# GpSimd's split of the chunks behind each half of a differential attention, held until VectorE's last weighted sum

## The chip, the cores and the metric

The kernel runs on one core of a Trainium2 chip. The metric is the device time of one launch in microseconds.

## The reference

Two transformer blocks are computed for 512 tokens of width 1024, all in float32. The first block has sliding-window attention, a gated delta rule, an MLP and a gated embedding. The second block has retention, differential attention, a merge by gates, an output projection, and a mixture of 32 experts with two per token. The change lies in the differential attention of the second block, whose core is:

```python
def block(args):
    i, qi = args
    s = jnp.einsum('bqhcd,bkhcd->bhcqk', qi, k).astype(jnp.float32) * scale
    qpos = i * Q_BLOCK + jnp.arange(Q_BLOCK)
    s = jnp.where(kpos[None, :] <= qpos[:, None], s, neg)
    p = jax.nn.softmax(s, axis=-1)
    a = p[:, :, 0] - lam * p[:, :, 1]
    return jnp.einsum('bhqk,bkhe->bqhe', a.astype(v.dtype), v)
```

There are 4 heads, each with two score matrices (c = 0, 1) of dk 128 and values of width 256, and four blocks of 128 queries. The queries, keys, values and two gates are projections of the same normalized input by `w_in_2` (1024 by 8192). After the attention, each head is normalized and multiplied by `w_diff_o_2`.

## The kernel before

**Weights in chunks.** Every dense product ("linear") of the first part of the kernel works on chunks of a weight matrix: 512 rows by 512 columns, laid out as 128 partitions by 2048 values, 1 MB. SyncE loads a chunk into one of three raw buffers (`load_chunk`, L233). Float32 precision comes from splitting each value into a high part and a low part: `split_chunk` does it on GpSimd, the high part `whi` at L241, and the low part `wlo` as raw minus high at L243. There are two buffers of `whi` and `wlo` (PAIR = 2). TensorE then makes three matmuls for each product (`three`, L264 to L266). In the MLP and some other places ScalarE and VectorE do the splits, but in the phase of the change GpSimd does all of them.

The order of chunks is fixed in one list. The load of chunk n waits until chunk n-3 is split. The split of chunk n waits until the load has landed and until TensorE is done with chunk n-2 (`used`), since it takes its buffer. `stream_split(pool, upto)` splits all chunks up to `upto + 2`, excluding that one, that have not been split yet.

**The differential attention** is done in two halves of two heads each. The chunks of a half are, in order: two for the queries FQ, two for the keys FK, two for the values FV (`U_dif[half][0]`), and then two for the gate (`gd_chunks[half]`); `U_dif[half][1]` is the index of the first gate chunk. Behind the gate chunks of the first half come FQ of the second, and behind those of the second half the four chunks of `w_diff_o_2` and then those of `w_out_2`.

In `attention(half)` each engine runs through eight units j = 0 to 7 (two heads, and in each four query blocks n = 0 to 3, with (n+1)*128 keys):

- TensorE: `scores` (one matmul for each of the two score matrices, into PSUM, L1958), issued two units ahead; pieces of the gate product, which use the two gate chunks, between units (done in unit 5); `turn` (n+1 transposes of the weighted probabilities, L1970), which waits for VectorE's weighted sum of this unit and for ScalarE's copy of the unit before; and after n = 3 `values` (16 matmuls, L1985).
- VectorE: `maxima`, one unit ahead: causal mask (L2146), maximum (L2149), scaling of two numbers per partition (L2151). Then for the unit itself: reciprocal of the sums (L2160), times lambda (L2162), first matrix scaled (L2163), and the weighted sum (L2166), which counts up the semaphore `dif` to step "a".
- ScalarE: exponentials one unit ahead (L2070), and behind them the copy of the turned probabilities out of PSUM (L2081); between units a copy of a gate tile (L2057). Its queue runs in order: the exponentials of unit j+1 stand before the copy of unit j.

Units count on through the halves: unit 7 of a half is `dif.at("a", 8 * half + 7)`.

When the units of the first half are done, TensorE goes on to the FQ linear of the second half, and behind the second half to the linear of `w_diff_o_2` (`U_do[0]`). Each begins with its first chunk: 48 matmuls, then the second chunk. The matmuls of the head's mean square (L2012) are put in after its first 12 matmuls. VectorE and ScalarE then normalize the half's heads (L1864 to L1879).

**Queues in this phase.** GpSimd's program is a single `stream_split(pool, out_end)`: it splits as soon as loads and buffers allow. SyncE loads the chunks up to the one behind the gate chunks, writes 16 blank blocks of 512 KB to `y_rows` (L1756), and goes on with loads.

Of the kernel before, what the change touches and what calls it, by code (L numbers as in the profile page):

```python
# [127 lines left out]
def build(nc, IN, out):  # L128
    ctx = ExitStack()
    with ctx:  # L130
# [14 lines left out]
        def late(name):  # L145

            late_sems.append(late_ctx.enter_context(nc.semaphore(name)))
            return late_sems[-1]
# [86 lines left out]
        def split_chunk(pool, n):  # L235
            _, rows, cols = chunks[n]
            w, r, s = rows * cols, n % RAW, n % PAIR
            pool.wait_ge(raw_full[r], 16 * (n // RAW + 1))
            if n >= PAIR:
                pool.wait_ge(*used[n - PAIR])  # L240
            nc.gpsimd.tensor_scalar(whi[:, s, 0:w], raw[:, r, 0:w], 1.0, 1.0, ALU.mult, ALU.mult).then_inc(split_hi, 1)  # L241
            pool.wait_ge(split_hi, n + 1)
            nc.gpsimd.tensor_tensor(wlo[:, s, 0:w], raw[:, r, 0:w], whi[:, s, 0:w].bitcast(F32),  # L243
                                    ALU.subtract).then_inc(split_done, 1)

        def chunk_high(act, n):

            _, rows, cols = chunks[n]
            w, r, s = rows * cols, n % RAW, n % PAIR
            act.wait_ge(raw_full[r], 16 * (n // RAW + 1))  # L250
            if n >= PAIR:
                act.wait_ge(*used[n - PAIR])
            nc.scalar.activation(whi[:, s, 0:w], raw[:, r, 0:w], ACT.Copy).then_inc(split_hi, 1)  # L253

        def chunk_low(dve, n):

            _, rows, cols = chunks[n]
            w, r, s = rows * cols, n % RAW, n % PAIR
            dve.wait_ge(split_hi, n + 1)
            nc.vector.tensor_tensor(wlo[:, s, 0:w], raw[:, r, 0:w], whi[:, s, 0:w].bitcast(F32), ALU.subtract).then_inc(split_done, 1)  # L260
# [107 lines left out]
        U_dif, U_gd, gd_chunks = [], [], []  # L368
# [27 lines left out]
        def stream_in(sp, upto_chunk):  # L396
            while issued[0] < min(upto_chunk + RAW, len(chunks)):
                load_chunk(sp, issued[0])
                issued[0] += 1

        def stream_split(pool, upto_chunk):
            while done_split[0] < min(upto_chunk + PAIR, len(chunks)):
                split_chunk(pool, done_split[0])
                done_split[0] += 1
# [92 lines left out]
        with phase() as block:  # L497
            @block.sync
            def _(sp):
                sp.dma_start(cbase[:], IN["k_base"][:, 0:4 * P]).then_inc(consts_in, 16)  # L500
                for t in range(TT):
                    sp.dma_start(x_tok[:, t, :], IN["x"][0, t * P:t * P + P, :]).then_inc(x_in, 16)
                stream_in(sp, 0)
# [1344 lines left out]
        dif = Steps(late("dif_dve"), "inv", "lam", "a0", "a")  # L1848
# [53 lines left out]
        with phase() as block:  # L1902
# [18 lines left out]

            @block.gpsimd
            def _(pool):
                stream_split(pool, out_end)

            @block.tensor
# [987 lines left out]
```

## Time and profile before

| | |
|---|---|
| median of 3 runs | 2122.1 us (2116.88, 2122.1, 2130.04) |
| profiled execution, own time | 2120.33 us |
| its span | 2118.5 us |
| mean granted TensorE clock | 0.969 |
| TensorE (PE) busy | 93%, 1974.1 us |
| VectorE (DVE) busy | 64%, 1361.0 us |
| ScalarE (ACT) busy | 44%, 939.1 us |
| GpSimd (POOL) busy | 25%, 534.8 us |
| DMA | 388.51 MB, mean 183 GB/s |

The span runs from the first to the last instruction in the profile; times in the rows are counted from its start. PEclk is the granted TensorE clock as a share of 2.4 GHz: 1.00 is 2.4 GHz and 0.50 is 1.2 GHz. A timeline row has the start, the duration, engine, line and operation, output<-inputs with shapes, the count of merged instructions, and in brackets the idle time of the engine just before it with what ended that. A wait row has who waited for whom, with the total, the count and the longest.

### The profile page before, as it was taken

The page shows a single profiled execution, that of the slowest core. Times are in us where ns is not written, and L with a number is a line of the kernel's source. Part 1 is how long each engine was busy: PE and PEld are TensorE (multiplying, and loading weights), DVE is VectorE, ACT ScalarE, POOL GpSimd, SP SyncE. Part 2 cuts the span into 40 slices and gives each one's busy share as a digit, 9 for nine tenths or more (in the row PEclk, how much of TensorE's full clock was granted, in tenths as well). Part 3 has the DMA queues.
Part 4 walks back from the last instruction along what each step waited for, and adds up shares of the span by engine and source line. Part 5 has one row for each costly group of instructions (what it writes and reads, how often), then busy time and mean ns, then how long its engine had stood idle before and what let it go on. Part 6 is the DMA issues. An engine that isn't in the chain of part 4 may idle for free. (4 is left out here: it accounts for less than half of the span.)

```text
span 2118.5 us, 24193 instructions
## 1 busy us (share of the span) xinstructions
PE 1974.1 (93%) x8966; PEld 1588.8 (75%) x8966; DVE 1361.0 (64%) x1393; ACT 939.1 (44%) x1029; POOL 534.8 (25%) x274
## 2 busy tenths in 40 slices
PE   3997898999999999999999897999999999999993
PEld 2875786888888877768877575778788787787882
DVE  4437874667665556524025446547799899999994
ACT  3113425423223452232002313325788888878883
POOL 2633003100000004516553353430022222222222
PEclk7998999999999999999999898998999999999996
DMA  4221001565563232243335153212899999999994
GB/s 146 96 90 60 21 14 40 189 194 200 173 207 135 96 93 74 69 160 100 100 99 219 42 185 131 79 64 111 302 376 373 364 363 366 367 378 375 371 363 152
DMA packets 115163, 388.51 MB, mean 183 GB/s; under 512 B 21333, under 2 KB 23668, under 8 KB 88334
## 3 DMA queue, kind: packets, MB, share of 16 engines
q1 hardware_dynamic: 98656, 353.00, 46.0%
q10 hardware_dynamic: 10382, 25.42, 3.6%
q0 software_dynamic: 6048, 9.03, 1.2%
q8 instruction: 52, 0.85, 0.2%
q14 instruction: 25, 0.20, 0.0%
HBM read 355.06 MB, written 45.35 MB: 189 GB/s over the span
## 5 line engine op out<-in xcount | busy, mean ns | idle before, releaser
L2832 DVE TENSOR_TENSOR m_lo<-m_raw,m_hi 128x2048 fp32r<-128x2048 f32 x200 | 449.1, 2286 | 9.4 <-ACT m_hi L2754 9.0
L2754 ACT ACTIVATE m_hi<-m_raw 128x2048 fp32r<-128x2048 f32 x200 | 383.1, 1922 | 105.1 <-DMA m_raw<-in_w_exp_gate_dram 67.0
L264 PE MATMUL ps<-xhi,whi 128*128 128x512 f32 x936 | 375.6, 401 | 11.8 <-DVE xlo L455 6.7
L265 PE MATMUL ps<-xlo,whi 128*128 128x512 f32 x936 | 366.2, 391 | 0.0
L266 PE MATMUL ps<-xhi,wlo 128*128 128x512 f32 x936 | 366.1, 391 | 0.0
L241 POOL TENSOR_SCALAR whi<-raw 128x2048 fp32r<-128x2048 f32 (+1 forms) x60 | 113.6, 1894 | 953.5 <-PE ps L266 874.9
L243 POOL TENSOR_TENSOR wlo<-raw,whi 128x2048 fp32r<-128x2048 f32 (+1 forms) x60 | 277.0, 4616 | 5.0
L264 PE MATMUL ps<-m_hi,xt_hi 128*128 128x512 f32 x544 | 218.6, 402 | 6.2 <-DVE xt_lo L2837 5.0
L264 PEld LDWEIGHTS ps<-xhi,whi 128*128 128x128 f32 x936 | 176.7, 189 | 57.4 <-issue 15.7
L265 PE MATMUL ps<-m_lo,xt_hi 128*128 128x512 f32 x544 | 215.7, 396 | 0.0
L266 PE MATMUL ps<-m_hi,xt_lo 128*128 128x512 f32 x544 | 214.0, 393 | 0.0
L265 PEld LDWEIGHTS ps<-xlo,whi 128*128 128x128 f32 x936 | 177.0, 189 | 39.2 <-issue 3.4
L266 PEld LDWEIGHTS ps<-xhi,wlo 128*128 128x128 f32 x936 | 176.8, 189 | 37.4
L264 PE MATMUL ps<-yhi,whi 128*128 128x512 f32 x448 | 175.8, 392 | 0.0
L266 PE MATMUL ps<-yhi,wlo 128*128 128x512 f32 x448 | 174.4, 389 | 0.0
L265 PE MATMUL ps<-ylo,whi 128*128 128x512 f32 x448 | 174.3, 389 | 0.0
L260 DVE TENSOR_TENSOR wlo<-raw,whi 128x2048 fp32r<-128x2048 f32 (+1 forms) x38 | 84.9, 2234 | 114.3 <-ACT whi L253 114.3
L253 ACT ACTIVATE whi<-raw 128x2048 fp32r<-128x2048 f32 (+1 forms) x38 | 70.9, 1867 | 167.5 <-PE ps L266 115.6
L264 PEld LDWEIGHTS ps<-m_hi,xt_hi 128*128 128x128 f32 x544 | 101.9, 187 | 32.5 <-issue 8.7
L266 PEld LDWEIGHTS ps<-m_hi,xt_lo 128*128 128x128 f32 x544 | 102.7, 189 | 24.2
L265 PEld LDWEIGHTS ps<-m_lo,xt_hi 128*128 128x128 f32 x544 | 102.5, 188 | 22.5
L2675 POOL TENSOR_TENSOR p_col<-p_col 128x1 f32<-128x1 f32 x34 | 47.2, 1388 | 283.8 <-ACT y_out L2773 283.8
(474 smaller groups left out, 3181.6 us busy)
## 6 DMA issues: line engine op xcount, KB each, us to landing
m_raw<-in_w_exp_gate_dram SPq DMA_DIRECT2D x68, 1024.0 KB, 5.9
m_raw<-in_w_exp_up_dram SPq DMA_DIRECT2D x68, 1024.0 KB, 6.4
m_raw<-in_w_exp_down_dram SPq DMA_DIRECT2D x68, 1024.0 KB, 5.9
raw<-in_w_in_dram SPq DMA_DIRECT2D x42, 1024.0 KB, 5.2
ada_w<-in_w_ada_dram ACTq DMA_DIRECT2D x48, 512.0 KB, 4.2
raw<-in_w_up_dram SPq DMA_DIRECT2D x16, 1024.0 KB, 5.7
raw<-in_w_down_dram SPq DMA_DIRECT2D x16, 1024.0 KB, 5.0
y_rows<-xhi SPq DMA_DIRECT2D x32, 512.0 KB, 11.4
```

Of the source, the lines that this page charges most:

```text
L241: nc.gpsimd.tensor_scalar(whi[:, s, 0:w], raw[:, r, 0:w], 1.0, 1.0, ALU.mult, ALU.mult).then_inc(split_hi, 1)
L243: nc.gpsimd.tensor_tensor(wlo[:, s, 0:w], raw[:, r, 0:w], whi[:, s, 0:w].bitcast(F32), ALU.subtract).then_inc(split_done, 1)
L253: nc.scalar.activation(whi[:, s, 0:w], raw[:, r, 0:w], ACT.Copy).then_inc(split_hi, 1)
L260: nc.vector.tensor_tensor(wlo[:, s, 0:w], raw[:, r, 0:w], whi[:, s, 0:w].bitcast(F32), ALU.subtract).then_inc(split_done, 1)
L264: nc.tensor.matmul(o, lh, rh, start=start, stop=False)
L265: nc.tensor.matmul(o, lh, rl, start=False, stop=False)
L266: return nc.tensor.matmul(o, ll, rh, start=False, stop=stop)
L2675: nc.gpsimd.tensor_tensor(p_col[:, 2:3], p_col[:, 0:1], p_col[:, 1:2], ALU.add)
L2754: nc.scalar.activation(m_hi[s][:], m_raw[s][:], ACT.Copy).then_inc(m_split, 1)
L2832: nc.vector.tensor_tensor(m_lo[s][:], m_raw[s][:], m_hi[s][:].bitcast(F32), ALU.subtract).then_inc(m_low, 1)
```

## The change

Before it splits everything up to the end of the phase, GpSimd goes through the two halves: it splits up to and including the two gate chunks of the half, and then waits until VectorE has made the weighted sum of unit 7 of that half. Only then does it go on to the chunks behind them: FQ of the second half behind the first, `w_diff_o_2` behind the second. All other engines' programs are as before.

```diff
--- before.py
+++ after.py
@@ -1921,6 +1921,9 @@
 
             @block.gpsimd
             def _(pool):
+                for half in range(2):
+                    stream_split(pool, U_dif[half][1])
+                    pool.wait_ge(*dif.at("a", 8 * half + 7))
                 stream_split(pool, out_end)
 
             @block.tensor
```

## Rows read from the trace of the kernel before

**Rows 1.** Waits of TensorE, whole span: total us, times, longest us
```profile
PE ps L1970 <- DVE dif_p L2166: 17.8, 2, 8.9
```

**Rows 2.** Timeline of VectorE, units 6 and 7: start us, us, engine, line
```profile
1175.52 1.23 DVE L2149 TENSOR_REDUCE dif_v<-ps 128x2 f32<-128x1024 f32 x1
1176.78 3.13 DVE L2151 TENSOR_SCALAR dif_v<-dif_v 128x2 f32<-128x2 f32 x1
...
1180.01 1.74 DVE L2162 TENSOR_TENSOR dif_v<-dif_v,small 128x1 f32<-128x1 f32 x1
...
1182.12 4.73 DVE L2166 SCALAR_TENSOR_TENSOR dif_p<-dif_p,dif_v 128x384 f32<-128x384 f32 x1
...
1187.55 0.75 DVE L2166 SCALAR_TENSOR_TENSOR dif_p<-dif_p,dif_v 128x512 f32<-128x512 f32 x1
```

**Rows 3.** Timeline of GpSimd, first half: three splits (of the third its start)
```profile
1173.35 1.90 POOL L241 TENSOR_SCALAR whi<-raw 128x2048 fp32r<-128x2048 f32 x1 [27.67 <-PE ps L266]
1175.33 4.55 POOL L243 TENSOR_TENSOR wlo<-raw,whi 128x2048 fp32r<-128x2048 f32 x1
1179.85 1.90 POOL L241 TENSOR_SCALAR whi<-raw 128x2048 fp32r<-128x2048 f32 x1
1181.83 4.60 POOL L243 TENSOR_TENSOR wlo<-raw,whi 128x2048 fp32r<-128x2048 f32 x1
1209.40 1.91 POOL L241 TENSOR_SCALAR whi<-raw 128x2048 fp32r<-128x2048 f32 x1 [22.97 <-PE ps L266]
```

**Rows 4.** Timeline of TensorE, first half: transposes of unit 7, value products, next linear
```profile
1188.48 1.09 PE L1970 MATMUL ps<-cbase,dif_p 128*128 128x128 f32 x4 [0.67 <-ACT dif_t L2081]
1190.25 6.31 PE L1985 MATMUL ps<-dif_t,fv 128*128 128x512 f32 x16 [0.69 <-ACT dif_t L2081]
1196.32 0.48 PE L264 MATMUL ps<-xhi,whi 128*128 128x512 f32 x1
```

**Rows 5.** Timeline of ScalarE, first half: gate copy, exponentials of unit 7
```profile
1178.32 0.59 ACT L2057 ACTIVATE gd_sig<-ps 128x512 f32<-128x512 f32 x1
1179.94 0.69 ACT L2070 ACTIVATE dif_p<-ps,dif_v 128x512 f32<-128x512 f32 x1 [1.03 <-DVE dif_v L2151]
...
1181.19 0.20 ACT L2070 ACTIVATION_READ_ACCUMULATOR dif_p<-ps,dif_v 128x1 f32 x1
```

**Rows 6.** Timeline of VectorE, then TensorE, units 2 and 3, without splits beside
```profile
1150.12 1.23 DVE L2149 TENSOR_REDUCE dif_v<-ps 128x2 f32<-128x1024 f32 x1
...
1152.17 0.62 DVE L2166 SCALAR_TENSOR_TENSOR dif_p<-dif_p,dif_v 128x384 f32<-128x384 f32 x1
...
1154.09 0.17 DVE L2160 RECIPROCAL dif_v<-dif_v 128x2 f32<-128x2 f32 x1 [0.29 <-ACT dif_p L2070]
...
1154.88 0.75 DVE L2166 SCALAR_TENSOR_TENSOR dif_p<-dif_p,dif_v 128x512 f32<-128x512 f32 x1
...
1158.83 0.60 PE L1970 MATMUL ps<-cbase,dif_p 128*128 128x128 f32 x4
1160.11 4.58 PE L1985 MATMUL ps<-dif_t,fv 128*128 128x512 f32 x16 [0.69 <-ACT dif_t L2081]
1164.45 0.47 PE L264 MATMUL ps<-xhi,whi 128*128 128x512 f32 x1
```

**Rows 7.** Timeline of TensorE, second half: transposes of unit 7, next linear
```profile
1320.12 1.08 PE L1970 MATMUL ps<-cbase,dif_p 128*128 128x128 f32 x4 [0.67 <-ACT dif_t L2081]
...
1328.68 0.48 PE L264 MATMUL ps<-yhi,whi 128*128 128x512 f32 x1
```

**Rows 8.** Windows: length, busy us of each engine, granted clock, DMA share, GB/s
```profile
342.00:344.00 2.00, 0.00 (x0) 0.00 (x0) 0.49 (x1) 1.95 (x3) 0.00 (x0) 0.96 0.00 0
1178.00:1187.00 9.00, 0.10 (x2) 0.10 (x2) 8.89 (x7) 2.32 (x6) 8.35 (x3) 0.62 0.38 117
```

**Rows 9.** DMA issues from 1120 to 1230 us: KB each, us to landing
```profile
y_rows<-xhi SPq DMA_DIRECT2D x16, 512.0 KB, 11.6
raw<-in_w_in_dram SPq DMA_DIRECT2D x7, 1024.0 KB, 5.3
```

## The prediction

> **What bounds the kernel now.** I read the page first: TensorE is busy for 93% of the span, so what counts is what TensorE waits for. The view of waits, for TensorE over the whole span, has one entry that belongs to this change: its transposes at L1970 wait 17.8 us in all, in two waits of up to 8.9 us, for VectorE's weighted sum at L2166 [rows 1]. Then I read each engine's timeline around the first of the two.
>
> In the first half VectorE does its last row of maxima over 512 columns at 1175.52 us. Then L2151, which touches 2 numbers per partition, takes 3.13 us and ends at 1179.91; L2162 takes 1.74 us and ends at 1181.75; the weighted sum of unit 6 takes 4.73 us and ends at 1186.85; that of unit 7 ends at 1188.30 [rows 2]. GpSimd works beside it: the low part (L243) that ends at 1179.88, the high part (L241) that ends at 1181.75, the next low part that ends at 1186.43 [rows 3]. VectorE's ends follow GpSimd's by 0.03, 0.00 and 0.42 us, and 0.42 us is what is left of a sum that by itself takes 0.62 us [rows 6]. So two engines that share no semaphore here end together three times. These GpSimd instructions are the splits of the two chunks behind the half, and the first of them was released by TensorE at 1173.35 [rows 3]: exactly what the change holds back. TensorE meanwhile is busy for 0.10 us of the 9 between 1178 and 1187 [rows 8]. What follows on it is a chain without slack: transposes of unit 6, of unit 7, the value products, then the next linear, which starts at 1196.32 [rows 4]. The second half repeats this 131.64 us later (1320.12 for 1188.48), and its next linear starts at 1328.68 [rows 4, 7].
>
> **The change, part by part.** It adds two waits on GpSimd; no instruction of work is added or removed. Per half, the two gate chunks are still split as before, since the helper splits two chunks beyond its argument. Behind each wait are queued the two splits above and all later ones; who needs them is TensorE's next linear, and SyncE's loads, which go by the count of splits.
>
> *The stall removed.* With GpSimd silent, unit 6's sum would end 2.67 us after the start of the 512-column maximum, as in unit 2 of the same half (1150.12 to 1152.79 [rows 6]), at 1178.2. That isn't what limits then. ScalarE's queue is next: its gate copy ends at 1178.91, and only behind it come the exponentials of unit 7, 1.45 us (1179.94 to 1181.39) [rows 5], to 1180.36. VectorE needs 0.04 us to start and 1.54 us from the reciprocal to the end of the sum (1154.09 to 1155.63 [rows 6]): unit 7's sum ends at 1181.94 in place of 1188.30. TensorE began 0.18 us after it [rows 2, 4], so its last transposes start at about 1182.0 in place of 1188.48: 6.48 us earlier. Unit 6's transposes and copy fit in before that.
>
> *From there to the next linear.* This depends on TensorE's clock. In the first half of the kernel before it took 1196.32 - 1188.48 = 7.84 us, in the second 1328.68 - 1320.12 = 8.56 us [rows 4, 7]. The same work for the first head of the half took 1164.45 - 1158.83 = 5.62 us [rows 6]; its value products took 4.58 us against 6.31 us [rows 4, 6]. The granted clock explains it: from 1178 to 1187 us, with hardly a matmul under way, the mean is 0.62, that is the engine began at 2.4 GHz and fell to 1.2 GHz [rows 8], and the value products began at the lower level. After the change TensorE still has about 5.3 us, from 1178.0 to the value products at 1183.3 (1.28 us behind the start of the last transposes, as in the first head [rows 6]), with unit 7's 0.60 us of transposes in them and the three of unit 6, some 1.1 us together. A pause of 2 us already brought the beginning of a fall (342 to 344 us, no matmul, mean 0.96 [rows 8]). So I expect the fall again, and take the stretch at its measured lengths: next linear at 1182.0 + 7.84 = 1189.8, or + 8.56 = 1190.6.
>
> By the Trainium skill, "TensorE: Matmul & The Clock Gate", Part 1, the clock goes by how busy the array has lately been and comes back only after sustained work. By that rule the fall is still to be expected here and the sum would be the 13 us below; if two short bursts of transposes kept the clock up, it would be the 15.7 us of the first rival. The rows decide it no further than that they show falls in pauses like this one.
>
> *The split that now comes late.* GpSimd starts when unit 7's sum is done. High and low part of one chunk take 6.58 us from start to end (1179.85 to 1186.43 [rows 3]); with 0.18 us to wake and 0.1 us to release TensorE the first chunk is there at 1181.94 + 6.86 = 1188.8. TensorE's own work covers it until 1189.8 in the slow-clock case, so it costs nothing; at the high clock TensorE would be there at 1182.0 + 5.62 = 1187.6 and wait 1.2 us. The second chunk is there at about 1195.4. TensorE needs it only when it is done with the first: 48 matmuls, and GpSimd's third split, which waits for just that, started at 1209.40 [rows 3], 13.1 us behind the linear's start. So it has until about 1202.9. VectorE has nothing to do in this time, so the splits run beside nobody. From the third split on everything hangs on the linear's start and moves with it. Bounds for the unseen cost of the wait: nothing, or 1.2 us a half; I take nothing.
>
> *Loads.* The load of the chunk five behind the first gate chunk is released by the delayed split, at about 1188.8; a load lands in 5.3 us [rows 9], and this chunk is split only behind the third split, which comes some 14 us after the release. Hidden.
>
> *Sum.* First half 6.5 us (1196.32 to 1189.8; 5.8 at the longer stretch). Second half, the same shift: 6.5 us with its own stretch of 8.56, 7.2 with 7.84. Together 12.3 to 13.7 us; if the clock falls late, so that the transposes still run fast and only the value products are slow, the start of the products is 0.5 us earlier in each half, up to 14.7. I take 13.5 us. All later stages hang on TensorE through these linears, so nothing absorbs it. The profiled execution took 2120.3 us (span 2118.5 and 1.8 around it): 2120.3 - 13.5 = 2106.8, say 2107. The median of the runs shown is 1.8 us higher, which would make 2108.6; the runs themselves lie 13 us apart, so I keep 2107.
>
> **The rivals.**
> 1. *The clock stays up.* The pauses are broken by transposes, and the longest, before those of unit 7, is about 3.0 us. Then the linears start when the split is done, at 1188.8 and 131.64 us later at 1320.4: 7.5 + 8.2 = 15.7 us, 2104.6; one half of the two gives 14.7. The new bound would be GpSimd's split. Against it: the fall that begins before 344 us, in a shorter pause.
> 2. *The stall doesn't go.* If VectorE's long instructions came from something else, unit 7's sum would still end at 1188.30, the split at 1195.2, and TensorE at 1196.3 would notice nothing: 2120. Against it: three coincident ends, the same in the second half.
> 3. *Slower: the raw chunk isn't there when GpSimd's wait ends*, so that a load stands on the path before L241. Break-even is when the first chunk is ready at 1196.3, 14.3 us after unit 7's sum; with 6.86 us for wait and split this decides at 7.5 us of loading. An ordinary load of 5.3 us would leave a gain of 2 to 3 us a half; one that takes the 11.6 us of the writes of y_rows on the same queue [rows 9] costs 4.1 us in the first half and 3.4 in the second, 7.5 in all: 2127.8. Against it: the split before was released by TensorE, not by a DMA [rows 3], so the chunk was already there, and nothing of SyncE's order changes.
>
> **How the numbers follow.** Forecast 0.58, rival 1 0.27, rival 2 0.10, rival 3 0.05. A measurement of this kernel tells about 1% (21 us) from no change. No case gives that much: the largest gain is 15.7 us, and only a spread of runs like the one shown could carry it over 21 us, 0.06. Slower by over 1% needs a load longer than 11.6 us: 0.02. Within 1%: 0.92. The forecast's own range is 2106 to 2108 by the terms; with rival 1 and the runs' scatter of a few us on both sides the range is 2100 to 2115; rivals 2 and 3 are left out.
>
> **What would show it.** Right: GpSimd's first split behind a half starts within 0.3 us of the end of unit 7's sum; no L2151, L2162 or L2166 in units 6 and 7 above 0.8 us; TensorE's waits for L2166 shrink from 17.8 us to below 3 us, and a wait for ScalarE's exponentials or of about 3 us before unit 7's transposes takes their place; clock rows below 1.0 again in the value products; last transposes to linear 7.8 to 8.6 us. It is wrong if the sums stay long with GpSimd silent, if TensorE waits at the linear for GpSimd's L243 by more than about 1 us, or if the gain at the linears is lost in a later stage.

## The result and the profile after

The changed kernel takes 2107.29 us, the median of 7 runs (2104.34 to 2115.27); the kernel before took 2120.05 us in the 7 runs beside them (2116.88 to 2130.04). The ratio is 0.9928 with a 95% interval of 0.9907 to 0.9949: by the ratio it is 15 us faster, within 11 to 20, which is less than 1%. The forecast was 2107.0 us. The profiled execution took 2113.64 us (span 2111.8).

The waits of TensorE over the whole span, which answer to [rows 1]; the columns are the total, the count and the longest. All lines behind L1923 have moved down by 3, so L1970 is now L1973 and the weighted sum L2166 is L2169:

```profile
PE ps L1973 <- DVE dif_p L2169: 5.6, 2, 2.8
```

17.8 us have become 5.6, in two waits of 2.8. VectorE's timeline for units 6 and 7 of the first half, which answers to [rows 2]:

```profile
1175.42 1.23 DVE L2152 TENSOR_REDUCE dif_v<-ps 128x2 f32<-128x1024 f32 x1
1176.68 0.17 DVE L2154 TENSOR_SCALAR dif_v<-dif_v 128x2 f32<-128x2 f32 x1
...
1177.48 0.62 DVE L2169 SCALAR_TENSOR_TENSOR dif_p<-dif_p,dif_v 128x384 f32<-128x384 f32 x1
1180.18 0.17 DVE L2163 RECIPROCAL dif_v<-dif_v 128x2 f32<-128x2 f32 x1 [2.09 <-ACT dif_p L2073]
...
1180.97 0.75 DVE L2169 SCALAR_TENSOR_TENSOR dif_p<-dif_p,dif_v 128x512 f32<-128x512 f32 x1
```

Every instruction has the length that it had in units 2 and 3 [rows 6]; the scaling took 0.17 us there too. The scaling of two numbers takes 0.17 us in place of 3.13, and the weighted sums take 0.62 and 0.75 us in place of 4.73 and 0.75. Unit 7's sum ends at 1181.72 us. The reciprocal at 1180.18 now waits 2.09 us for ScalarE. GpSimd, which answers to [rows 3]:

```profile
1181.81 1.90 POOL L241 TENSOR_SCALAR whi<-raw 128x2048 fp32r<-128x2048 f32 x1 [36.22 <-DVE dif_p L2169]
1183.79 4.50 POOL L243 TENSOR_TENSOR wlo<-raw,whi 128x2048 fp32r<-128x2048 f32 x1
1188.26 1.90 POOL L241 TENSOR_SCALAR whi<-raw 128x2048 fp32r<-128x2048 f32 x1
1190.24 4.58 POOL L243 TENSOR_TENSOR wlo<-raw,whi 128x2048 fp32r<-128x2048 f32 x1
1202.84 1.91 POOL L241 TENSOR_SCALAR whi<-raw 128x2048 fp32r<-128x2048 f32 x1 [8.01 <-PE ps L266]
```

The first split starts 0.09 us behind the sum and ends at 1188.29, the second ends at 1194.82, the third starts at 1202.84, when TensorE has released the first chunk. TensorE in the first half, from the transposes of unit 5 on, which answers to [rows 4]:

```profile
1177.52 0.38 PE L1973 MATMUL ps<-cbase,dif_p 128*128 128x128 f32 x2
1178.46 0.52 PE L1973 MATMUL ps<-cbase,dif_p 128*128 128x128 f32 x3 [0.56 <-ACT dif_t L2084]
1181.78 1.11 PE L1973 MATMUL ps<-cbase,dif_p 128*128 128x128 f32 x4 [2.79 <-DVE dif_p L2169]
1183.58 6.41 PE L1988 MATMUL ps<-dif_t,fv 128*128 128x512 f32 x16 [0.69 <-ACT dif_t L2084]
1189.74 0.48 PE L264 MATMUL ps<-xhi,whi 128*128 128x512 f32 x1
```

The next linear starts at 1189.74 with no wait of its own: the split was there 1.45 us earlier. The value products still take 6.41 us. The windows show why; their columns are those of [rows 8]:

```profile
1178.00:1182.00 4.00, 0.74 (x4) 0.54 (x5) 1.56 (x5) 2.53 (x7) 0.19 (x1) 0.81 0.00 0
1182.00:1186.00 4.00, 3.31 (x7) 1.66 (x7) 0.00 (x0) 0.60 (x1) 3.92 (x2) 0.50 0.02 4
1186.00:1188.00 2.00, 2.00 (x7) 1.35 (x6) 0.00 (x0) 0.00 (x0) 2.00 (x1) 0.67 0.00 0
1188.00:1190.00 2.00, 2.00 (x9) 1.34 (x8) 0.00 (x0) 0.00 (x0) 2.00 (x2) 1.00 0.31 48
```

The clock falls to 1.2 GHz before 1182 us, in the pause of 2.79 us ahead of unit 7's transposes, and is back at 2.4 GHz by 1188; the products run without a gap from 1183.58 on, so the first of them run at the lower level. ScalarE's queue, which answers to [rows 5], shows what now comes last before unit 7's sum, the gate copy and then the exponentials:

```profile
1178.22 0.59 ACT L2060 ACTIVATE gd_sig<-ps 128x512 f32<-128x512 f32 x1
1178.69 0.69 ACT L2073 ACTIVATE dif_p<-ps,dif_v 128x512 f32<-128x512 f32 x1
```

**Where the time went, by stages.** One length is used in all that follows: from the start of unit 5's transposes (the ones with two per group, L1970 or L1973) to the start of the next linear. It was 18.70 us in the first half of the kernel before (1177.62 to 1196.32) and 19.42 in the second; it is 12.22 (1177.52 to 1189.74) and 12.76 us (1302.71 to 1315.47) in the changed one. A second length runs from that same point of the first half to the mixture's first load. It was 1426.59 - 1177.62 = 248.97 us and is 1413.42 - 1177.52 = 235.90 us: 13.07 us less, of which the two halves give 6.48 and 6.66. So nothing between the attention and the mixture takes anything back. The row of unit 5's transposes in the kernel before, from TensorE's timeline, and then its loads, from SyncE's queue:

```profile
1177.62 0.38 PE L1970 MATMUL ps<-cbase,dif_p 128*128 128x128 f32 x2
...
1426.59 0.90 SPq L2319 DMA_DIRECT2D m_raw<-in_w_exp_gate_dram  x2
...
1488.74 3.13 SPq L2319 DMA_DIRECT2D m_raw<-in_w_exp_up_dram  x2
...
2059.68 0.44 SPq L2661 DMA_DIRECT2D mod_g<-mod_hold  x1
```

The loads of the changed kernel:

```profile
1413.42 0.91 SPq L2322 DMA_DIRECT2D m_raw<-in_w_exp_gate_dram  x2
...
1475.53 3.10 SPq L2322 DMA_DIRECT2D m_raw<-in_w_exp_up_dram  x2
...
2052.80 0.43 SPq L2664 DMA_DIRECT2D mod_g<-mod_hold  x1
```

The mixture itself, from its second group of loads (behind a stretch of 59 us without loads) to the load of its gate, took 577.27 us in this execution (1475.53 to 2052.80) and 570.94 in that of before (1488.74 to 2059.68). That is why the profiled spans differ by only 6.7 us while the medians differ by 12.8. Two of the runs below look at this.

### The profile page after: what moved, and what is told of

It reads as the page before. It is cut to its first block and busy times, and to the rows that moved or that the text cites. A ratio compares the mean times of both kernels' runs of the same rounds, so it can differ in the third digit from the quotient of the medians.

```text
span 2111.8 us, 24193 instructions
## 1 busy us (share of the span) xinstructions
PE 1980.2 (94%) x8966; PEld 1593.8 (75%) x8966; DVE 1343.4 (64%) x1393; ACT 939.0 (44%) x1029; POOL 533.1 (25%) x274
## 5 line engine op out<-in xcount | busy, mean ns | idle before, releaser
L260 DVE TENSOR_TENSOR wlo<-raw,whi 128x2048 fp32r<-128x2048 f32 (+1 forms) x38 | 84.9, 2234 | 114.2 <-ACT whi L253 114.2
L253 ACT ACTIVATE whi<-raw 128x2048 fp32r<-128x2048 f32 (+1 forms) x38 | 71.0, 1867 | 167.4 <-PE ps L266 115.6
L264 PE MATMUL ps<-m_hi,ht_hi 128*128 128x512 f32 x272 | 107.2, 394 | 1.8 <-ACT y_out L2776 1.8
```

The costliest lines, as they stand in the source:

```text
L264: nc.tensor.matmul(o, lh, rh, start=start, stop=False)
```

## The experiments

There were twelve runs beside the two of the comparison: ten other kernels, and each of the two once more. "Half 1" and "half 2" are the first length, "to mixture" the second, "products" the value products of unit 7 in the two halves, "mixture" the length of the mixture as just given. The ratio is to the runs of the kernel before beside them. A kernel is "filled" where matmuls whose result nobody reads stand in one of TensorE's pauses. The cuts of code show only the lines in question, against the changed kernel, or against the kernel before where no wait on GpSimd is in it; "..." marks lines left out.

| kernel | half 1 | half 2 | products | to mixture | mixture | ratio (95%) |
|---|---|---|---|---|---|---|
| before | 18.70 | 19.42 | 6.31, 7.03 | 248.97 | 570.9 | |
| changed | 12.22 | 12.76 | 6.41, 6.95 | 235.90 | 577.3 | 0.9928 (0.9907 to 0.9949) |
| first wait alone | 12.18 | 19.44 | 6.36, 7.05 | 242.49 | 577.7 | 0.9968 (0.9951 to 0.9985) |
| second wait alone | 18.71 | 12.71 | 6.33, 6.90 | 242.36 | 574.2 | 0.9959 (0.9944 to 0.9973) |
| wait for the products | 18.50 | 18.43 | 6.28, 6.21 | 251.81 | 575.5 | 1.0021 (1.0002 to 1.0040) |
| wait for unit 6 | 22.07 | 22.80 | 6.28, 7.01 | 255.75 | 566.9 | 1.0027 (1.0009 to 1.0046) |
| changed, pause filled | 10.83 | 10.84 | 4.58, 4.58 | 232.59 | 576.2 | 0.9925 (0.9905 to 0.9945) |
| the same, gate copy late | 10.35 | 10.35 | 4.58, 4.58 | 231.63 | 572.7 | 0.9937 (0.9917 to 0.9958) |
| split on idle engines | 9.45 | 9.45 | 4.58, 4.58 | 229.79 | 572.4 | 0.9915 (0.9889 to 0.9941) |
| before, 8 behind unit 6 | 24.02 | 23.80 | 4.58, 4.58 | 258.73 | 568.2 | 1.0056 (1.0032 to 1.0081) |
| before, 8 behind unit 5 | 18.81 | 19.38 | 6.50, 7.27 | 249.10 | 573.4 | 0.9982 (0.9962 to 1.0003) |
| before, 10 behind unit 5 | 16.43 | 16.44 | 4.58, 4.58 | 244.05 | 572.6 | 0.9994 (0.9972 to 1.0016) |
| before, again | 18.80 | 19.46 | 6.40, 7.06 | 249.16 | 567.1 | 1.0003 (0.9983 to 1.0023) |
| changed, again | 12.12 | 12.71 | 6.31, 6.90 | 235.72 | 573.5 | 0.9932 (0.9902 to 0.9962) |

In both kernels that were run twice the length up to the mixture repeats within 0.2 us, and the halves within 0.1, so these lengths resolve what the whole kernel's time, which scatters by 9 to 20 us between runs of one kernel, doesn't.

**One wait alone, in either half.**

```diff
-                for half in range(2):
-                    stream_split(pool, U_dif[half][1])
-                    pool.wait_ge(*dif.at("a", 8 * half + 7))
+                stream_split(pool, U_dif[0][1])
+                pool.wait_ge(*dif.at("a", 7))
                 stream_split(pool, out_end)
```

> Only the first half's wait. Read as the time from the start of unit 5's transposes to the start of the next linear (before: 18.70 us in the first half, 19.42 in the second; changed kernel: 12.22 and 12.82). Theory (GpSimd's split stretches VectorE's small instructions): first half 12 to 12.5, second half still 19 to 19.8, whole kernel 6.5 us below before. Rival (something else in the changed order shortens both, or the stall of the second half depends on the first): second half also changes. Rival (a later stage takes part of it back): less than 6.5 at the start of the mixture's loads.

> Only the second half's wait. Theory: first half still 18 to 19 us from unit 5's transposes to the next linear, second half 12.5 to 13.2; the start of the mixture's loads 6.6 us earlier than before; whole kernel 6.6 us below before, and with the run of the first half alone the two gains add up to the changed kernel's. Rival: the two do not add up.

In the second of them the index is 1 and the unit 15. Each wait shortens its own half and leaves the other as it was: 12.18 and 19.44, 18.71 and 12.71. To the mixture they save 6.48 and 6.61 us, 13.09 together, against 13.07 for both. The ratios give 6.8 and 8.7 us, and 15 for both. The halves are independent and add up, as the theory had it. (The expectation gives 12.82 us for the changed kernel's second half; its trace has 12.76.)

**The wait put later, behind the value products.**

```diff
-                    pool.wait_ge(*dif.at("a", 8 * half + 7))
+                    pool.wait_ge(dif_value, 2 * half + 2)
```

> The wait is put later: GpSimd goes on only when the half's last value products are done. Nothing covers the split then, and TensorE should stand at the next linear for 0.2 + 6.5 + 0.1 = 6.8 us in each half. Theory (the split in the changed kernel is covered by the last transposes and value products): from unit 5's transposes to the next linear 12.2 + 6.8 = 19.0 us and 12.8 + 6.8 = 19.6, so the kernel lies at before's time, within 1 us. A pause this long should also pull the clock down again at the linear's start, at 1 to 2.5 us more a half, so up to 5 us slower than before. Rival (the split is not what the next linear needs): time as the changed kernel.

TensorE's timeline at the next linear of the first half:

```profile
1182.00 6.28 PE L1988 MATMUL ps<-dif_t,fv 128*128 128x512 f32 x16 [0.69 <-ACT dif_t L2084]
1194.90 0.80 PE L264 MATMUL ps<-xhi,whi 128*128 128x512 f32 x1 [6.62 <-POOL wlo L243]
```

Now TensorE stands for GpSimd's low part, 6.62 us in each half. So the split is indeed what the next linear needs, and in the changed kernel it is the products that cover it. The clock comes down again in this wait, as expected: it is granted at 1.00 from 1188 to 1192 us and at a mean of 0.59 from 1192 to 1195. The window behind the linear's start:

```profile
1195.00:1199.00 4.00, 4.00 (x10) 3.14 (x11) 0.00 (x0) 0.00 (x0) 3.92 (x2) 0.50 0.74 220
```

The halves were expected at 19.0 and 19.6 us and came out at 18.50 and 18.43: the transposes of unit 7 ran at the high clock in both, in 0.66 us, and in the second half the products took 6.21 us in place of 6.95. But to the mixture it is 2.84 us more than before although the halves are 0.20 and 0.99 us shorter, so 4.0 us are lost behind the linears' starts, which begin at 1.2 GHz. Held until nothing covers the split, the same wait loses what it had gained: the kernel is at 1.0021 (1.0002 to 1.0040) of the kernel before.

**The wait put earlier, at unit 6's sum.**

```diff
-                    pool.wait_ge(*dif.at("a", 8 * half + 7))
+                    pool.wait_ge(*dif.at("a", 8 * half + 6))
```

> The wait is put earlier: GpSimd goes on at the weighted sum of unit 6, about 3.7 us before that of unit 7. Theory (an instruction of VectorE with operands in SBUF stands until GpSimd's instruction ends): the first low part runs from about 1180.1 to 1184.6 us; unit 7's reciprocal or product before it stretches to that end, the sum of unit 7 ends at about 1186 in place of 1181.7, possibly later if it meets the second split too, and the next linear starts 4 to 7 us later than in the changed kernel in each half. Rival (VectorE is only slowed in proportion, or only the long weighted sums suffer): less than 1 us later. Rival (the early split helps, since it is done sooner): faster than the changed kernel.

VectorE from unit 7's reciprocal on, and GpSimd beside it, in the first half:

```profile
1179.94 0.17 DVE L2163 RECIPROCAL dif_v<-dif_v 128x2 f32<-128x2 f32 x1 [2.09 <-ACT dif_p L2073]
1180.14 4.29 DVE L2165 TENSOR_TENSOR dif_v<-dif_v,small 128x1 f32<-128x1 f32 x1
1184.36 2.21 DVE L2166 TENSOR_SCALAR dif_p<-dif_p,dif_v 128x512 f32<-128x512 f32 x1
1186.60 4.86 DVE L2169 SCALAR_TENSOR_TENSOR dif_p<-dif_p,dif_v 128x512 f32<-128x512 f32 x1
```

```profile
1177.94 1.90 POOL L241 TENSOR_SCALAR whi<-raw 128x2048 fp32r<-128x2048 f32 x1 [32.61 <-DVE dif_p L2169]
1179.92 4.50 POOL L243 TENSOR_TENSOR wlo<-raw,whi 128x2048 fp32r<-128x2048 f32 x1
1184.39 1.90 POOL L241 TENSOR_SCALAR whi<-raw 128x2048 fp32r<-128x2048 f32 x1
1186.37 4.54 POOL L243 TENSOR_TENSOR wlo<-raw,whi 128x2048 fp32r<-128x2048 f32 x1
```

Three instructions in a row stand: the product of one number per partition for 4.29 us, to 1184.43, where the low part ends at 1184.42; the scaling of the first matrix to 1186.57, past the end of the high part at 1186.29; the weighted sum to 1191.46, past the end of the next low part at 1190.91. One number per partition stands as long as a matrix, so it is no slowing in proportion. The second half shows the same three lengths, 4.29, 2.21 and 4.86 us. I had expected the sum at 1186 or later; it met the second split too and came at 1191.46. The halves take 22.07 and 22.80 us: 3.4 us longer each than with no wait at all, and the kernel is slower than before by 0.27%. In the kernel before unit 6's sum took the worst of it, and unit 7 was free; here, with the splits started 3.6 us earlier than in the changed kernel, the whole of unit 7 behind its reciprocal is caught.

The prediction named no rival in which the DMA traffic that runs beside the splits holds VectorE up. The windows settle it. They lie within the scaling of 3.13 us in the kernel before, and within the product of 4.29 us in this one:

```profile
1176.80:1179.80 3.00, 1.20 (x7) 0.75 (x5) 3.00 (x1) 0.87 (x2) 3.00 (x1) 1.00 0.00 0
```

```profile
1180.20:1184.40 4.20, 0.00 (x0) 0.00 (x0) 4.20 (x2) 0.09 (x1) 4.20 (x2) 0.85 0.00 0
```

The DMA share, the last column but one, is 0.00 in both, while VectorE and GpSimd are busy from end to end.

By the Trainium skill, "SBUF — State Buffer", "SBUF: two separate sides", VectorE and GpSimd share a pair of ports to SBUF as an exclusive lock, held for the whole instruction. The three ends here agree with it. That page names VectorE's instructions with two inputs in SBUF or in a two-port mode. The rows fit: the product and the weighted sum have two such inputs and stood, and the reciprocal at 1179.94, which has one and ran within the low part, took its usual 0.17 us. The scaling has one input and stood too; by that page this takes the two-port mode, and no row here shows in which mode it ran.

**TensorE's pause filled.** Three matmuls go in before unit 7's transposes; their result is read by nobody and they are no part of the computation.

```diff
                         turn(j)
+                        if j == 6:
+                            pe.wait_ge(dif_exp, 2 * (i0 + 7))
+                            for _ in range(3):
+                                nc.tensor.matmul(ps[:, SB, :], ident, fk[:, 0, :], start=True, stop=True)
```

> The changed kernel, and TensorE fills the pause before unit 7's transposes with three matmuls whose result nobody reads (some 2.8 us at 2.4 GHz). Theory (the value products run at 1.2 GHz only because of the pause): the granted clock stays at 1.0 and the products take 4.6 us, not 6.4 and 6.95; TensorE then stands for GpSimd's first split, since this is ready at 6.8 us after unit 7's sum: next linear 1.0 to 1.5 us earlier than in the changed kernel in the first half, 1.5 to 2 in the second, 2.5 to 3.5 us in all, and a wait for L243 of about 1 us. Rival (the clock falls for another reason): products as long as before and nothing gained. Rival (the filling delays unit 7's transposes): up to 0.5 us a half lost.

```profile
1183.60 2.74 PE L2008 MATMUL ps<-fk,cbase 128*128 128x512 f32 x6
1186.56 0.66 PE L1973 MATMUL ps<-cbase,dif_p 128*128 128x128 f32 x4 [0.21 <-DVE dif_p L2173]
1187.90 4.58 PE L1988 MATMUL ps<-dif_t,fv 128*128 128x512 f32 x16 [0.69 <-ACT dif_t L2088]
1193.13 0.50 PE L264 MATMUL ps<-xhi,whi 128*128 128x512 f32 x1 [0.65 <-POOL wlo L243]
```

The granted clock is 1.00 from 1183 to 1196 us, the products take 4.58 us in both halves, and TensorE stands 0.65 and 0.66 us for the low part. The halves are 1.39 and 1.92 us shorter than in the changed kernel, 3.31 us in all to the mixture. So in the changed kernel the pause is what brings the clock down, and with it gone GpSimd's split is the bound, as the first rival of the forecast said. The whole kernel's ratio (0.9925) can't tell this from the changed kernel (0.9928).

**The clock in the kernel before.** Three tries with the same unread matmuls and no wait on GpSimd; in the first j is 6 and there are 8, in the second and third j is 5 and there are 8 and 10.

```diff
                         turn(j)
+                        if j == 5:
+                            pe.wait_ge(dif_exp, 2 * (i0 + 7))
+                            for _ in range(10):
+                                nc.tensor.matmul(ps[:, SB, :], ident, fk[:, 0, :], start=True, stop=True)
```

> The kernel before, with no wait on GpSimd, and the 8.9 us pause filled with eight matmuls whose result nobody reads (7.5 us at 2.4 GHz). It takes the clock's share by itself. Theory: VectorE's long instructions stay (3.1, 1.7 and 4.7 us), the clock stays at 1.0, the stretch from unit 7's transposes to the next linear shrinks from 7.84 and 8.56 us to 5.6, so 2.2 + 2.9 = 5 us faster than before in all. Rival (the low clock is no consequence of the pause): no change.

This one was put in the wrong place: in the kernel before the long pause lies ahead of unit 6's transposes, not behind them, so the eight matmuls stood on the path for 8.58 us and the kernel got slower. One reading it gives all the same: with them, unit 7's transposes to the linear took 1203.92 - 1198.30 = 5.62 us.

> The kernel before, without a wait on GpSimd, with the eight unread matmuls now where its 8.9 us pause is: behind the transposes of unit 5, before those of unit 6 (in the run with them behind unit 6 they came after the pause, on the path). Theory (the pause brings the clock down): VectorE's long instructions stay, the value products take 4.6 us, and from unit 5's transposes to the next linear it takes 18.70 - 0.4 - 2.2 = about 16 us in the first half and 19.42 - 0.4 - 2.9 = about 16 in the second. From the first half's unit 5 to the mixture's first load some 5.5 us less than before's 248.97. Rival (the clock is low for another cause): 18.7 and 19.4 as before.

```profile
1179.31 7.03 PE L2005 MATMUL ps<-fk,cbase 128*128 128x512 f32 x16
1188.39 0.63 PE L1970 MATMUL ps<-cbase,dif_p 128*128 128x128 f32 x3 [2.05 <-DVE dif_p L2170]
1189.84 1.12 PE L1970 MATMUL ps<-cbase,dif_p 128*128 128x128 f32 x4 [0.83 <-DVE dif_p L2170]
1191.64 6.50 PE L1985 MATMUL ps<-dif_t,fv 128*128 128x512 f32 x16 [0.69 <-ACT dif_t L2085]
```

```profile
1188.00:1190.00 2.00, 0.79 (x4) 0.47 (x5) 1.71 (x5) 0.49 (x1) 0.00 (x0) 0.68 0.44 72
```

Nothing was gained. Eight matmuls took 7.03 us and left a pause of 2.05, and the products took 6.50 us in the first half and 7.27 in the second. By an estimate from the mean clock of windows that hold the change of level, it fell in the first half 0.3 us behind the pause (0.68 from 1188 to 1190), and in the second, behind a pause of the same length, only 1.7 us behind it (0.71 from 1321 to 1323), when unit 7's transposes were under way. So the fall doesn't come at a fixed distance from the pause.

> As the run with eight unread matmuls behind unit 5 in the kernel before, but with ten, some 8.8 us, so that nothing of the first pause is left. With eight a pause of 2.05 us stayed, and the value products ran at 1.2 GHz (6.50 and 7.27 us). Theory (a pause of 2 us followed by short transposes with waits between them is enough for the low clock): value products 4.6 us, unit 7's transposes to the next linear 5.6 us, so 16.5 us from unit 5's transposes to the next linear in both halves, and 244 us from unit 5 to the mixture's first load (before 248.97). Rival (in the kernel before the clock falls for a cause other than the pause): 18.7 and 19.4 again.

```profile
1177.11 8.75 PE L2005 MATMUL ps<-fk,cbase 128*128 128x512 f32 x20
1186.19 0.55 PE L1970 MATMUL ps<-cbase,dif_p 128*128 128x128 f32 x3 [0.34 <-DVE dif_p L2170]
1187.64 0.66 PE L1970 MATMUL ps<-cbase,dif_p 128*128 128x128 f32 x4 [0.91 <-DVE dif_p L2170]
1188.98 4.58 PE L1985 MATMUL ps<-dif_t,fv 128*128 128x512 f32 x16 [0.69 <-ACT dif_t L2085]
1193.32 0.48 PE L264 MATMUL ps<-xhi,whi 128*128 128x512 f32 x1
```

With ten the pause is 0.34 us, the products take 4.58 us, and the halves 16.43 and 16.44, to the mixture 244.05, as expected. The granted clock is 1.00 in every window from unit 5's transposes to the linear, with gaps of 0.34, 0.91 and 0.69 us. So of the kernel before the clock's share was 2.3 and 3.0 us a half. The ratio of this kernel, 0.9994 (0.9972 to 1.0016), doesn't show the 4.9 us; in its profiled execution the stage from the mixture's first load to its second group of loads took 66.6 us in place of 62.1. The changed kernel got none of it: it takes away 6.5 us of standing and leaves a pause that still costs the clock. By the Trainium skill, "TensorE: Matmul & The Clock Gate", Part 1, activity releases the clock and idleness throttles it; these runs agree with that, and here a pause of 2.05 us with short transposes behind it was already followed by the fall.

**ScalarE's queue.** Two unread matmuls, and the copy of the last gate tile (L2060) behind the copy of unit 6.

```diff
-                        elif j == 5:
+                        elif j == 6:
                             gate_out(half, 3)
```

> The changed kernel with the pause filled by two matmuls and, on ScalarE, the last gate tile's copy moved from before unit 7's exponentials to behind the copy of unit 6. Theory (unit 7's exponentials, and with them its sum and GpSimd's start, hang on ScalarE's queue): they start about 0.5 us earlier, sum, split and next linear with them; together with the fuller clock 1.5 to 2 us a half below the changed kernel, 3 to 4 us in all. Rival (the exponentials wait for something else): nothing beyond what the filled pause gives, 2.5 to 3.5 us.

Both halves take 10.35 us, 0.48 less than with the pause filled alone. Unit 7's exponentials begin 0.70 us behind unit 5's transposes (1186.44 for 1185.74) and not 1.17 (1183.47 for 1182.30), so they did hang on that copy. That there are two unread matmuls here and three there takes no part in it: in both TensorE waits for unit 7's sum behind them, 0.59 and 0.21 us. To the mixture the kernel is 4.27 us below the changed one, a little more than the 3 to 4 expected; its ratio, 0.9937, doesn't show it.

**The first split on the engines that are idle.** ScalarE makes the high part behind the copy of unit 6, VectorE the low part behind unit 7's sum, with the helpers that the MLP uses (`chunk_high`, L253; `chunk_low`, L260). The two unread matmuls stay. `done_split` is the program's own count of split chunks: raised by one, it makes GpSimd leave that chunk out and go on when the others have split it.

```diff
-                        elif j == 5:
+                        if j == 6:
+                            chunk_high(act, U_dif[half][1] + 2)
+                        elif j == 7:
                             gate_out(half, 3)
...
+                    chunk_low(dve, U_dif[half][1] + 2)
...
                     stream_split(pool, U_dif[half][1])
-                    pool.wait_ge(*dif.at("a", 8 * half + 7))
+                    done_split[0] += 1
+                    pool.wait_ge(split_done, done_split[0])
```

> The first chunk behind each half is no longer split by GpSimd but by two engines that stand idle then: ScalarE makes the high part behind the copy of unit 6, VectorE the low part behind the sum of unit 7; GpSimd goes on when that is done. The last gate copy stands behind the copy of unit 7, and two unread matmuls fill TensorE's pause. Theory (what is left behind the changed kernel's sum is GpSimd's 6.5 us and a pause with low clock): chunk ready 2.5 to 3 us after the sum, TensorE goes to the linear without a wait: 9.4 us from unit 5's transposes to the next linear in both halves (changed kernel 12.22 and 12.76, kernel with the late gate copy 10.35), and 229.5 to 230 us from unit 5 of the first half to the mixture's first load (changed 235.9). Rival (the new work on ScalarE's or VectorE's queue delays the copy of unit 7 or the sum): 10.3 us or more.

```profile
1187.88 0.75 DVE L2176 SCALAR_TENSOR_TENSOR dif_p<-dif_p,dif_v 128x512 f32<-128x512 f32 x1
1189.27 2.29 DVE L260 TENSOR_TENSOR wlo<-raw,whi 128x2048 fp32r<-128x2048 f32 x1 [0.64 <-ACT whi L253]
```

```profile
1190.03 4.58 PE L1989 MATMUL ps<-dif_t,fv 128*128 128x512 f32 x16 [0.69 <-ACT dif_t L2089]
1194.37 0.48 PE L264 MATMUL ps<-xhi,whi 128*128 128x512 f32 x1
```

The chunk is there at 1191.56, 2.9 us behind the sum's end at 1188.63, and TensorE goes from the products into the linear with nothing between. The halves take 9.45 us each, so 9.3 and 10.0 us less than before, and 229.79 us to the mixture: 19.2 us less than before and 6.1 less than the changed kernel. The ratio, 0.9915 (0.9889 to 0.9941), beats the kernel before; against the changed kernel run beside it (0.9932, 0.9902 to 0.9962) the intervals overlap, so there only the stage shows it ahead.

**Both kernels once more.**

> The kernel before, once more, for a second trace of it. If the mixture's length (from the second group of its loads to the gate's load at its end: 570.9 us before, 577.3 in the changed kernel) differs only from execution to execution, this one may lie anywhere in 567 to 578. If the changed kernel makes the mixture longer, it lies at 571 within 2 us. From unit 5 to the mixture's first load: 249.0 within 0.3.

> The changed kernel once more. Scatter of executions: mixture anywhere in 567 to 578 us. The change at fault: 577 within 2 us. From unit 5 to the mixture's first load 235.9 within 0.6 (the clock may come back one step earlier or later). Ratio to before 0.993 to 0.994.

Up to the mixture they repeat: 249.16 us and 235.72. The mixture took 567.1 and 573.5 us. The changed kernel's was not at 577 again and the kernel before's not at 571: each moved by 4 us on its own, and over all kernels it lies between 566.9 and 577.7, the longest one in a kernel with only one wait. So most of the difference seen in the profiled pair is scatter. The kernel with the wait at unit 6, which has both waits too, had the shortest of all, 566.9. But in both pairs the changed kernel's mixture was the longer by 6 us, and two pairs can't exclude that a part of it is real. The ratios speak against a large part: both (0.9928, 0.9932) are at or beyond the 13.1 us, which would be 0.9938, though the interval of the second (to 0.9962) alone would leave room for 5 us.

## Why the prediction was right

- *The cause of the stall* was read rightly from three coincident ends; that DMA traffic could be the cause was not considered, and the windows above exclude it for two of the stalls. The length of each instruction went back to that of units 2 and 3, and the run with the wait one unit earlier made the stall return in another place.
- *What is late next* was ScalarE's gate copy, the exponentials and VectorE's chain, as said. The exponentials were put at 1178.91 and began at 1178.69, unit 7's sum at 1181.94 and ended at 1181.72. The trace of after starts the stage 0.10 us earlier; the rest is that ScalarE's instructions overlap by 0.1 us.
- *Unit 7's transposes* were put at 1182.0 and came at 1181.78. One reading there was wrong without harm: the 0.18 us between the sum's end and the transposes was taken for the time that a release needs. The row itself says that they waited for ScalarE's copy [rows 4]; behind the sum they start after 0.06 us. The addition slipped as well, since 1181.94 + 0.18 is 1182.12 and not 1182.0; with the 0.06 it comes to 1182.0, so the two errors cancel.
- *The clock* fell again in both halves. The stretch from these transposes to the linear was put at 7.84 to 8.56 us; it took 7.96 (1181.78 to 1189.74) and 8.50 (1306.97 to 1315.47). The pause at 342 us that was called 2 us is one of 2.37 us in TensorE's timeline (to 344.01).
- *The split covered*: put at 1188.8, it was there at 1188.29, 1.45 us before TensorE needed it. The terms of 0.18 us to wake and 0.1 to release were taken too long: GpSimd started 0.09 us behind the sum, and with the pause filled TensorE started 0.05 us behind the low part (1193.08 to 1193.13). The third split came 13.10 us behind the linear's start, as before.
- *The sum*: 13.5 us forecast, 13.07 measured to the mixture's first load, with 6.5 and 6.5 to 7.2 for the halves against 6.48 and 6.66. The whole kernel went from 2120.05 to 2107.29. That the median lies 0.3 us from the forecast is luck: the runs lie 11 us apart, and the same kernel's median was 2116.12 us when it was run again (beside 2126.52 for the kernel before). What was forecast well is the gain, not the absolute time.
- *The first rival* (clock stays up) did not happen, but the run with the filled pause shows it as described: the split becomes the bound, at 10.83 us for a half, with TensorE waiting 0.65 us for it and not 1.2. It would have given 16.4 us to the mixture against the 15.7 of the forecast's sum. The second and third rivals fell: the sums shortened, and GpSimd's first split behind each half was released by VectorE, not by a load.
- *A marker that was badly put*: TensorE's wait for the weighted sum was to shrink below 3 us with another wait of about 3 us in its place. The new wait is put down to the same pair of lines, twice 2.8 us, so the group shows 5.6.

## What to carry to other kernels

Where a trace shows an instruction on a few numbers taking microseconds, compare its end with the ends of the other engine's instructions before looking at semaphores; VectorE and GpSimd working on SBUF at once can stall a short critical chain with no wait in any program. When such work of GpSimd starts matters: of the three places tried here the best was the one behind VectorE's chain that the following work still covered. One unit earlier cost 10 us a half, and one step later 6 us, or 8 with what the low clock cost behind it. Better still was to give the first chunk to two engines that stood idle (9.45 us for a half in place of 12.22 and 12.76). When a stall is removed, read the clock after it separately: the pause that is left may still bring it down. Judge small gains by the length of the stage and not by the whole kernel's time.

## What the runs showed of the hardware

- VectorE's maximum over PSUM and its reciprocal kept their length beside GpSimd's low part (1.23 us for the maximum in [rows 2] and in [rows 6], 0.17 us for the reciprocal in the run with the wait at unit 6), while one product of one number per partition stood for 4.29 us.
- In the kernel before with the pause filled, a pause of 2.05 us with sparse transposes behind it was followed by TensorE's fall to 1.2 GHz in both halves; with gaps of 0.34, 0.91 and 0.69 us the clock stayed at 2.4 GHz in both.
- One and the same mixture took 567 to 578 us in fourteen executions, and the stage between its first and second group of loads took 62.1 to 62.2 us in ten of them, but 63.6 to 66.6 in four.
